# The next head's latent key projection moved from the inverse's levels into the scan's first step

## What is computed

```python
k = silu(short_conv(h @ W_k)); v, q likewise      # 512 latent tokens, 256 context tokens
lmat = strict_lower((k*beta) @ k.T * decay)       # per chunk
sol = triangular_solve(lmat + I, [v*beta, k*beta*exp(gc)])   # the inverse
for chunk in order:                               # the scan
    v_new = u - w @ S;  S = S*exp(g_last) + k_dec.T @ v_new
    o = q_dec @ S + attn @ v_new
```

## Time and profile before

| | |
|---|---|
| median of the runs | 2092.33 us |
| span of the profiled execution | 2089.2 us |
| TensorE matmul busy | 2030.5 us, 97% of the span |
| VectorE, ScalarE, GpSimd busy | 72%, 45%, 46% |
| granted TensorE clock, mean | 0.992 of full speed |
| heads' stage (inverse and scan, 8 heads) | about 97.9 to 596.5 us |

### The profile page before, as it was taken

How to read it: one execution, slowest core, us unless ns; L and a number is a source line. 1 busy time by engine, 2 the same in 40 slices (tenths; PEclk the granted TensorE clock), 3 DMA queues, 4 the chain that set the end, 5 groups by cost and what they waited for, 6 DMA issues and landing times.

```text
span 2089.2 us, 39445 instructions
## 1 busy us (share of the span) xinstructions
PE 2030.5 (97%) x13974; PEld 1793.9 (86%) x13974; DVE 1495.3 (72%) x3294; ACT 934.7 (45%) x1687; POOL 955.9 (46%) x585
## 2 busy tenths in 40 slices
PE   5899999999999998999999999999999999999997
PEld 2788888888787887889999999999998888888886
DVE  5777777777651117678979867777549888888888
ACT  3544444434343234333343478888643333333332
POOL 0413343223424447545899966666763322222222
PEclk9899999999999999999999999999999999999999
DMA  7323222223213345434688879999999999999993
GB/s 274 108 78 106 77 87 92 96 77 107 74 42 110 100 151 181 142 103 128 200 297 268 277 271 351 368 358 366 379 367 375 384 365 344 366 343 360 352 356 121
DMA packets 151781, 470.06 MB, mean 225 GB/s; under 512 B 15632, under 2 KB 46576, under 8 KB 148464
## 3 DMA queue, kind: packets, MB, share of 16 engines
q1 hardware_dynamic: 108064, 300.13, 41.4%
q0 software_dynamic: 36864, 134.23, 17.6%
q10 hardware_dynamic: 6736, 34.08, 4.0%
HBM read 415.38 MB, written 53.00 MB: 224 GB/s over the span
## 4 chain that ended last, share of the span: by engine, by line
PE 87%; DVE 5%; POOL 3%; DMA 2%; ACT 1%; issue 1%; SPq 1%; POOLq 0%; ACTq 0%; DVEq 0%
PE bank L2910 24%; PE bank L589 13%; PE bank L591 13%; PE bank L590 13%; PE bank L2897 4%; POOL w_lo L1277 2%; PE pair L589 2%; PE bank L2503 2%; PE bank L2493 2%; PE pair L590 1%; PE pair L591 1%; DMA rows<-peer_u,e_row 1%; PE bank L2325 1%; PE bank L2466 1%; PE pair L2466 1%
## 5 line engine op out<-in xcount | busy, mean ns | idle before, releaser
L1277 POOL TENSOR_TENSOR w_lo<-raw,w_hi 128x1024 fp32r<-128x1024 f32 x148 | 363.5, 2457 | 498.3 <-ACT w_hi L789 269.1
L589 PE MATMUL bank<-lat_hi,w_hi 128*128 128x384 f32 (+2 forms) x1488 | 535.5, 360 | 4.2 <-DVE lat_lo L1993 2.6
L591 PE MATMUL bank<-lat_hi,w_lo 128*128 128x384 f32 (+2 forms) x1488 | 521.1, 350 | 0.0
L590 PE MATMUL bank<-lat_lo,w_hi 128*128 128x384 f32 (+2 forms) x1488 | 520.4, 350 | 0.0
L589 PEld LDWEIGHTS bank<-lat_hi,w_hi 128*128 128x128 f32 x1488 | 280.6, 189 | 19.0 <-issue 4.8
L591 PEld LDWEIGHTS bank<-lat_hi,w_lo 128*128 128x128 f32 x1488 | 280.0, 188 | 17.9
L590 PEld LDWEIGHTS bank<-lat_lo,w_hi 128*128 128x128 f32 x1488 | 280.7, 189 | 13.4 <-issue 0.2
L1397 POOL DMA_INDIRECT rows<-peer_v,e_row x128 | 135.9, 1062 | 338.0 <-DVE pair L2211 318.1
L1277 POOL TENSOR_TENSOR w_lo<-raw_more,w_hi 128x1024 fp32r<-128x1024 f32 x80 | 199.7, 2499 | 94.0 <-ACT w_hi L1014 65.0
L2910 PE MATMUL bank<-w_lo,c_hi 128*128 128x512 f32 x768 | 237.1, 389 | 0.0
L2910 PE MATMUL bank<-w_hi,c_hi 128*128 128x512 f32 x768 | 237.1, 389 | 0.0
(11 more groups left out here) (398 smaller groups left out, 3603.4 us busy)
## 6 DMA issues: line engine op xcount, KB each, us to landing
raw<-w SPq DMA_DIRECT2D x210, 512.0 KB, 4.0
raw_more<-w SPq DMA_DIRECT2D x142, 512.0 KB, 4.7
g_dram<-gs ACTq DMA_DIRECT2D x24, 1024.0 KB, 8.8
gu_dram<-gu SPq DMA_DIRECT2D x120, 192.0 KB, 5.6
gq<-g_dram SPq DMA_DIRECT2D x45, 512.0 KB, 8.3
gl<-gu_dram SPq DMA_DIRECT2D x28, 768.0 KB, 7.5
ada<-w_ada SPq DMA_DIRECT2D x32, 512.0 KB, 4.2
dY<-gc_dram SPq DMA_DIRECT2D x8, 768.0 KB, 4.3
```

The lines of the kernel that those rows point to most:

```text
L589: nc.tensor.matmul(out, hi, rh, start=start, stop=False)
L590: nc.tensor.matmul(out, hi, rl, start=False, stop=False)
L591: return nc.tensor.matmul(out, lo, rh, start=False, stop=stop)
L1277: nc.gpsimd.tensor_sub(w_lo[:, slot, :], raw_at(slot % 2 if src is None else src), w_hi[:, slot, :].bitcast(F32)).then_inc(split_done, 1)
```

## The change

The call that runs K_LAT blocks inside the levels is removed, with its table, and the first four entries of the fill table change: K_LAT goes whole into the first two places of step 0, K_CTX into the two after that.

```diff
-                    if h < H - 1:
-                        project(h + 1, K_LAT, K_EARLY[lv])
...
-            K_EARLY = ((), (0, 1), (2,), (), (3,), (4,), (5,))
             SCAN_FILL = (
-                ((K_LAT, 6, 8),), ((K_CTX, 0, 3),), ((K_CTX, 3, 5),),
-                ((K_CTX, 5, 8),), ((V_LAT, 0, 2),), ((V_LAT, 2, 4),),
+                ((K_LAT, 0, 4),), ((K_LAT, 4, 8),), ((K_CTX, 0, 4),),
+                ((K_CTX, 4, 8),), ((V_LAT, 0, 2),), ((V_LAT, 2, 4),),
```

## The result

The changed kernel takes 2109.03 us, the median of four runs (2105.94 to 2110.95), against 2092.6 us for the kernel before in four runs (2091.68 to 2093.23): 1.0077 times as long, interval 1.0063 to 1.0091. The span of its profiled execution is 2107.3 us. The prediction said 2110.0, range 2105 to 2116, span 2107.0. It was right in sign and in size, but by the traces the size is partly luck: the heads cost 14.3 us where it had added up 17.8. Two of its terms were off, and in the profiled execution stages after the heads took longer and made up for them. Of its own signs, the inverse came out at 18.55 us and not at 18.8 to 19.0, and the period grew by 2.25 us, where "a period that is not 2.6 longer" was to count against it.

The account below looks back on a forecast made before the run. TensorE, busy 97% of the span, was taken as the bound. Six heads at 4.20 - 1.6 = 2.6 us plus head 0's 2.2 gave 17.8, span 2107.0, with 3.1 around it 2110 us; range 2105 to 2116.

Parts of the forecast that it names:

- a period that is not 2.6 longer: Sign against the forecast: a head's period, first solve to first solve, was to go from 63.1 to 65.7 us.
- What the scan's first steps get: Scan's step 0: six moved blocks at 0.70 us cost 4.20 us a head; line 2503 to step 2's products grows 11.44 to 15.6.
- What leaves the inverse: Inverse of heads 1 to 6 without its six blocks: gives back 1.58 to 1.69 us a head, taken as 1.6.
- the reading of head 7 as a clean sample: Head 7's inverse, run without K_LAT blocks (18.84 us against head 6's 20.53), taken to show the changed inverse.
- The loop's price on the taps: VectorE's chain in level 2: taps 2 and 3 take 1.61 us in the loop of heads 1 to 6, 1.50 outside.
- Head 0: Head 0's inverse, begun at the lower clock: gives back 2.0 us, from 1.5 to 2.2, out of 20.12.
- The late convolution: Rival, 12%: tap 0 holds up the new state and solve 1 waits, 0.3 to 0.8 us a head, 2112 to 2116 us.
- VectorE's delay: Scan up to solve 1: VectorE delayed 4.26 us, TensorE 4.20, ending within 0.15 us of each other, so no wait.
- The rival that work is only moved: Rival, 4%: TensorE's total busy time and so the time stay the same, 2092 us; needs an inverse of 16.3 us.
- Faster: Rival, 2%: blocks and five insertions between 64x64 groups come back whole from the inverse, 12 us less, 2080.
- The rival that head 0 stays at the lower clock: Rival, 4%: gaps in head 0's inverse keep TensorE at 1.2 GHz longer, 5 to 8 us, 2115 to 2118.
- The sum: All heads: 2.6 us for each of heads 1 to 6, 2.2 for head 0, 17.8 us together; nothing after the heads.

## Why the prediction held, and what in it did not

*What the scan's first steps get* was right: 4.20 us predicted, 4.21 measured, 11.44 to 15.65 us (predicted 15.6). It is made of two things, though: six blocks of 0.68 us and 0.14 of waiting. In the fill of four the blocks of head 0 start at 116.87, 117.56 and 118.24 and the solve at 118.92, 0.68 to 0.69 each; the 0.70 that I used came from the second block of a fill of two.

*What leaves the inverse* was off by a term. Predicted 1.6, measured 1.98. By level the inverse of head 6 gives back 0.88 in level 1 (3.91 to 491.55 - 488.52 = 3.03) and 0.71 in level 6 (1.79 to 507.07 - 505.99 = 1.08), both as predicted to the hundredth. Levels 2 to 5 give back 0.39 (14.83 to 505.99 - 491.55 = 14.44) instead of 0.10, all of it in level 5, which takes 2.91 us before (the two rows below, head 6) and 505.00 - 502.48 = 2.52 after. Emptying level 5 alone confirmed it.

```profile
490.94 0.52 PE L2466 MATMUL pair<-Xh,Lt 64*64 64x64 f32 x12
...
493.85 0.27 PE L2466 MATMUL pair<-Xh,Lt 64*64 64x64 f32 x2
```

The step that failed is the reading of head 7 as a clean sample. TensorE's rows in level 4 of head 7, kernel before:

```profile
551.61 0.56 PE L2493 MATMUL bank<-T,W 64*64 64x64 f32 x12 [0.81 <-DVE T L1696]
552.00 0.52 PE L2503 MATMUL bank<-W,T 64*64 64x64 f32 x12
552.35 0.52 PE L2493 MATMUL bank<-T,W 64*64 64x64 f32 x12
553.04 0.56 PE L2503 MATMUL bank<-W,T 64*64 64x64 f32 x12 [0.17 <-issue]
553.44 0.52 PE L2466 MATMUL pair<-Xh,Lt 64*64 64x64 f32 x12
```

The groups of 12 start 0.35 apart, but the fourth comes 0.69 after the third, with a wait for nothing that the profile shows. The stretch from 551.61 takes 1.83 us here, 1.44 in head 6 of after (501.04 to 502.48). This 0.38 is a stall of one execution and not head 7's own: the step from head 6 to head 7 is 62.75 us in the profile of before and 62.33 to 62.35 in those of the eight kernels whose code between these two solves is the same (all with K_LAT in no other place of the scan than the first). The inverse of head 7, whose work no edit changes, takes 18.44 to 18.46 us in the 13 other profiles, and 18.84 in this one. The stall hid what level 5 gives back. One other of the 14 profiles has such a gap, in level 2 of head 6 with levels 2 and 4 emptied; there the wait for Xh behind it was shorter by as much (0.43 instead of 0.83), and the period stayed at 64.42. What causes it is open. The loop's price on the taps, which I took off, was real: without the stall head 7 needs 14.35 where the loop needs 14.44.

*Head 0*: predicted 2.0 with a high end of 2.2, measured 2.86 (20.12 to 17.26). TensorE's rows of head 0 after; compare:

```profile
97.90 0.90 PE L2466 MATMUL pair<-Xh,Lt 64*64 64x64 f32 x12
98.60 0.90 PE L2466 MATMUL bank<-Xh,Lt 64*64 64x64 f32 x12
99.46 0.91 PE L2491 MATMUL bank<-T,W 64*64 64x64 f32 x12
100.13 0.71 PE L2501 MATMUL bank<-W,T 64*64 64x64 f32 x12
100.67 0.53 PE L2491 MATMUL bank<-T,W 64*64 64x64 f32 x12
101.02 0.53 PE L2501 MATMUL bank<-W,T 64*64 64x64 f32 x12
101.37 0.53 PE L2466 MATMUL pair<-Xh,Lt 64*64 64x64 f32 x12
...
115.16 0.97 PE L2501 MATMUL bank<-XTh,T 64*64 64x64 f32 x24
```

Level 1 takes 3.47 us instead of 5.14 and so gives back 1.67, where I allowed 1.3 at most; levels 2 to 5 give 0.42 and level 6 gives 0.77. There is no wait in level 1 here: at the lower level of the clock (1.2 GHz) TensorE's own first products take 1.56 us (97.90 to 99.46), and by then T and W are there. So the two blocks covered nothing. Before, they took 2.16 us (99.39 to 101.55), the first at the lower level; now the four groups behind them run partly at it instead, 1.91 us (99.46 to 101.37) against 1.45 (101.55 to 103.00), and the rest comes back. The groups then shorten from 0.70 to 0.35, to the upper level (2.4 GHz), at the same time as before the change (by 101 us), with the blocks or without: between 100 and 101 us the mean granted clock is 0.67 of full speed in the profile of before and 0.74 in that of after, and 1.00 from there on. This is one pair of executions. Over all 14 profiles level 1 of head 0 takes 4.40 to 5.14 us with two blocks and 2.99 to 3.84 with none, as the clock rises earlier or later in it, so what head 0 gives back can't be told to better than several tenths.

*The rivals.* The late convolution was the right mechanism and existed from the start: 0.14 us a head, as one place for all of K_LAT shows, under the 0.3 to 0.8 that I gave it, and 1.04 with K_LAT one place later. Its room was not 0.15 but less than nothing at solve 1, and about 0.7 at the products with the state, which I had not looked at. VectorE's delay was foretold to 0.01 us: from the start of line 2503 to the second residual's end 7.74 us in head 6 of before and 12.01 after, 4.27 more (4.26 predicted). TensorE's was not, 4.08 and not 4.20 (7.74 to 11.82 for solve 1), since six blocks cost 0.68 each. So VectorE came out 0.19 behind TensorE where the prediction had 0.06. The rival that work is only moved fell (the inverse is 18.55, not 16.3). Faster fell for the same reason. The rival that head 0 stays at the lower clock fell too, by the rows above.

*The sum.* Predicted 2.6 x 6 + 2.2 = 17.8 us; the heads cost 14.3 (15.67 - 1.41). The error of 3.5 us is 6 x 0.38 from the stall that was taken for a property of the inverse, 0.86 from head 0, and 0.4 from the same stall once more: it lengthens head 7 in the profile of before (18.84 against 18.45 us after), and the sum had nothing to set against it. The span agreed to 0.3 us all the same, since in this profile the late part was 3.8 us longer, which I had put at nothing. That agreement is luck. The medians, less open to that, differ by 16.4 us and 16.1. The heads in the traces account for 14.3 of it, or 14.7 without the stall. The other 1.5 us or so are not explained; the intervals, 13 to 19 us, do not ask for them.

## What to carry to other kernels

Independent work that is put into a wait is free only as long as that wait is, so price every place by itself, by the stage's length with and without it: here taking a block of 0.68 us out of a level gave back between 0.0 and 0.71 us, depending on the level. Once priced one at a time, the prices added up to within 0.03 us a head, and a mix that no single run had tried came out as computed. A second block in the same place has a price of its own (0.26 to 0.70).

An iteration that lacks the filler in the old kernel is a free sample of the new one, and here it gave the answer. But one iteration of one profile may hold a stall of its own: look for a gap inside a stream that should be even, before its length is believed.

When work moves past a shared in-order queue, follow the consumer's place in that queue to whoever comes next, at each of the following uses and not only at the one that seemed tight.

## What was not expected of the hardware

A late part of the kernel that no edit touched took from 1527.0 to 1531.4 us in 14 profiled executions. The inverse of head 0, the first place that an edit touches, began between 97.05 and 102.73 us. The kernel's time contains both swings, so a change of a few tenths of a us a head is seen in the periods (63.06 against 63.08) long before it is seen in the time.
